# Turning x2 and the gated values: squares of 32 on VectorE and DMAs in runs of 128 B in place of TensorE transposes

## The chip, the cores and the metric

One core of a Trainium2 chip runs the whole program. The metric is the device time of one execution in microseconds (us). "PE" is TensorE, "DVE" is VectorE, "ACT" is ScalarE, "POOL" is GpSimd and "SP" is SyncE, whose queue issues most DMAs.

## The reference, cut to what matters

One layer of a hybrid decoder in float32, 512 positions and 2048 channels: norm, one wide projection, attention and RWKV-7 heads, a gated merge, then

```python
    x = x + merged @ w_out[l]                                   # x2
    h = rms_norm(x, norm_ffn[l])
    x = x + (jax.nn.silu(h @ ffn_gate[l]) * (h @ ffn_up[l])) @ ffn_down[l]
    return rms_norm(x, norm_final)
```

`FFN_HIDDEN` is 5632. The change concerns what stands between these products: x2 (the first line's sum) and the gated values silu(..) * (..) have to be turned, one with channels on the partitions into positions on the partitions, the other the opposite way, because a matmul contracts over the partitions.

## The kernel before, in words

**Precision.** Each float32 product is made of three matmuls: an operand is split by ACT into a rounded high part and by DVE or POOL into the low rest, and high x high, high x low and low x high are summed in PSUM.

**The output projection.** 16 tiles of 128 channels (m = 0 to 15), 48 matmuls of 128x512 each. For a tile, POOL makes the low part of the weights (`low_part`), DVE adds the residual (`residual`, L1708) into one of two x2 buffers, ACT scales and squares it, and DVE builds the sums that the FFN needs. PE then turns the tile in four 128x128 transposes (`turn_x2`, L2399), ACT copies the bank to `xt` and writes it to `sum_dram` (`turned_x2`, L1089), which holds the residual with positions on the partitions; the end of the FFN is added there.

**The FFN.** It is computed by a scheme of seven products of half-size blocks, in the order (1, 7, 5, 6, 2, 3, 4), with sums before and after. There are 11 chunks of 512 hidden columns (j = 0 to 10: gate and up), then 6 passes for the down product (j = 11 to 16). In a chunk each product has 8 steps (k), a step is six matmuls of 128x512 (`gate_up_items`, L2419). For every step ACT writes `ring_hi` (`ring_high`, L1055) and DVE `ring_lo` (`ring_low`, L1752); these rings are four deep, and ACT may refill a place only when PE has done the step four before. All queues are programs written out by hand in this order; nothing is scheduled by a tool. I write (5,3) for product 5, step 3.

**The weights.** SP loads four blocks of 2 MB per chunk (`load_block`, L665). POOL issues two further DMAs of 1 MB per chunk that add one block onto another in memory (L791); they start when DVE has made `ring_lo` for (7,3) and (7,7), and product 6 needs them.

**The seam.** While chunk j runs, the results of chunk j - 1 are finished: silu by ACT, the product by DVE (`hidden1` L1801 at the end of the chunk, `hidden2` L1813 in product 7 of the next). These values stand in three buffers of 128x2x512, `u2buf`, `u3buf` and `c22buf`, as positions x hidden columns. PE turns them in 8 transposes after product 4 (`u2buf`) and 8 more after (7,3) of the next chunk (`c22buf`), ACT copies the four banks back (`turned1_out`, `turned2_out`), DVE makes four sums (`s_of_hidden`, L1819), and SP stores the seven operand blocks to `s_dram` in four DMAs. The three buffers are used again by the running chunk: ACT copies product 1 to `u2buf` at (6,4) and (6,5), DVE writes `u3buf` in product 2.

**The down passes.** `s_dram` is read back, 1 MB for each operand block, by `load_s` (L677) at j = 10, 12 and 14, and split by ACT and DVE (`split_s`, `s_low`) in the product after.

## Time and profile before

| | |
|---|---|
| median of 3 runs | 2778.48 us (2775.72 to 2781.59) |
| the profiled execution, its own time | 2777.86 us |
| its span | 2776.0 us |
| PE busy | 2730.2 us |
| DVE, ACT, POOL busy | 1798.3, 1267.3, 639.2 us |
| data moved by DMA | 382.51 MB in 190611 packets |

The span is the time from the first to the last instruction in the profile; what lies around it is 1.9 us. Busy PE time counts matmuls that overlap, so the distance between the starts of two matmuls says more than the length of one.

### The profile page before, as it was taken

How to read it: one execution, taken by the hardware profiler on the slowest of the kernel's cores; microseconds unless marked ns; L12 is line 12 of the kernel's file. 1: busy time of each engine (PE TensorE's matmuls, PEld its weight loads, DVE VectorE, ACT ScalarE, POOL GpSimd, SP SyncE). 2: the span in 40 equal slices, each digit the busy share in tenths (PEclk: the TensorE clock that was granted, in tenths of full speed). 3: DMA queues.
4: the chain of work that ended last, by engine and by line, in shares of the span. 5: the costliest groups of instructions: out<-in, count | busy, mean ns of one | idle time of the engine just before them, and what ended most of it. 6: DMA issues, size and time to landing. Idle time of an engine off the chain costs nothing.

```text
span 2776.0 us, 37866 instructions
## 1 busy us (share of the span) xinstructions
PE 2730.2 (98%) x14290; PEld 2204.4 (79%) x14290; DVE 1798.3 (65%) x2947; ACT 1267.3 (46%) x2110; POOL 639.2 (23%) x487
## 2 busy tenths in 40 slices
PE   8999999999999999999999999999999999999997
PEld 7777777777777777888887888888888888888876
DVE  5656365364463554432258878887788789888886
ACT  5444343343333334222345555555555556556555
POOL 2323234243333343554440000000000000111112
PEclk9999999999999999999999999999999999999999
DMA  5222122222222223443445665446545677787784
GB/s 189 76 76 105 64 84 94 76 88 79 76 84 83 78 97 110 160 155 129 136 132 160 178 178 153 143 160 178 145 130 162 178 215 213 190 255 179 197 215 109
DMA packets 190611, 382.51 MB, mean 138 GB/s; under 512 B 9584, under 2 KB 84592, under 8 KB 175728
## 3 DMA queue, kind: packets, MB, share of 16 engines
q1 hardware_dynamic: 145808, 319.76, 33.3%
q0 software_dynamic: 29728, 45.09, 9.9%
q10 hardware_dynamic: 14912, 15.47, 1.6%
q8 instruction: 103, 1.69, 0.2%
q14 instruction: 60, 0.49, 0.1%
HBM read 328.91 MB, written 51.38 MB: 137 GB/s over the span
## 4 chain that ended last, share of the span: by engine, by line
PE 91%; DVE 3%; ACT 2%; issue 1%; DMA 1%; DVEq 1%; POOL 0%; ACTq 0%; SPq 0%; POOLq 0%
PE dense L2037 12%; PE work L2430 11%; PE work L2432 11%; PE work L2434 11%; PE dense L2039 11%; PE dense L2038 11%; PE dense L2430 3%; PE dense L2432 3%; PE dense L2434 3%; PE work L2205 1%; PE work L2443 1%; PE work L2257 1%; ACT whi L821 1%; DVEq L1313 1%; PE work L2037 1%
## 5 line engine op out<-in xcount | busy, mean ns | idle before, releaser
L821 ACT ACTIVATE ring_hi<-wblock 128x512 fp32r<-128x512 f32 x840 | 529.7, 632 | 526.0 <-PE work L2434 350.2
L759 POOL TENSOR_TENSOR wlo<-raw,whi 128x512 fp32r<-128x512 f32 x400 | 541.1, 1383 | 896.4 <-ACT whi L821 896.4
L1756 DVE TENSOR_TENSOR ring_lo<-wblock,ring_hi 128x512 fp32r<-128x512 f32 x840 | 575.9, 689 | 166.5 <-ACT ring_hi L821 157.7
L2430 PE MATMUL work<-ring_hi,S_hi 128*128 128x512 f32 x1460 | 572.0, 392 | 6.9 <-DVE ring_lo L1756 6.8
L2432 PE MATMUL work<-ring_hi,S_lo 128*128 128x512 f32 x1460 | 568.9, 390 | 0.0
L2434 PE MATMUL work<-ring_lo,S_hi 128*128 128x512 f32 x1460 | 568.8, 390 | 0.0
L2037 PE MATMUL dense<-H_hi,whi 128*128 128x512 f32 x1208 | 504.8, 418 | 10.0 <-DVE H_lo L1341 8.5
L2039 PE MATMUL dense<-H_hi,wlo 128*128 128x512 f32 x1208 | 473.2, 392 | 0.0
L2038 PE MATMUL dense<-H_lo,whi 128*128 128x512 f32 x1208 | 473.0, 392 | 0.0
L821 ACT ACTIVATE whi<-raw 128x2048 fp32r<-128x2048 f32 (+1 forms) x109 | 198.2, 1821 | 473.7 <-PE dense L2039 388.3
L2430 PEld LDWEIGHTS work<-ring_hi,S_hi 128*128 128x128 f32 x1460 | 274.4, 188 | 69.5 <-DVE ring_lo L1756 7.3
L2434 PEld LDWEIGHTS work<-ring_lo,S_hi 128*128 128x128 f32 x1460 | 274.5, 188 | 57.2
L2432 PEld LDWEIGHTS work<-ring_hi,S_lo 128*128 128x128 f32 x1460 | 274.6, 188 | 55.7
L2037 PEld LDWEIGHTS dense<-H_hi,whi 128*128 128x128 f32 x1208 | 227.6, 188 | 81.7 <-issue 27.0
L2039 PEld LDWEIGHTS dense<-H_hi,wlo 128*128 128x128 f32 x1208 | 227.4, 188 | 49.9
L2038 PEld LDWEIGHTS dense<-H_lo,whi 128*128 128x128 f32 x1208 | 228.0, 189 | 44.8 <-issue 5.8
L791 POOL DMA_DIRECT2D wblock<-w_gu x22 | 28.4, 1290 | 799.3 <-DVE ring_lo L1756 799.3
L2430 PE MATMUL dense<-ring_hi,S_hi 128*128 128x512 f32 x388 | 153.0, 394 | 2.4 <-DVE ring_lo L1756 2.1
L2432 PE MATMUL dense<-ring_hi,S_lo 128*128 128x512 f32 x388 | 151.1, 389 | 0.0
L2434 PE MATMUL dense<-ring_lo,S_hi 128*128 128x512 f32 x388 | 151.1, 389 | 0.0
L2037 PE MATMUL dense<-M_hi,whi 128*128 128x512 f32 x256 | 101.1, 395 | 0.0
L2039 PE MATMUL dense<-M_hi,wlo 128*128 128x512 f32 x256 | 99.8, 390 | 0.0
(337 smaller groups left out, 3409.4 us busy)
## 6 DMA issues: line engine op xcount, KB each, us to landing
raw<-w_slots SPq DMA_DIRECT2D x101, 1024.0 KB, 4.9
wblock<-w_gu SPq DMA_DIRECT2D x88, 1024.0 KB, 9.7
wblock<-w_down SPq DMA_DIRECT2D x60, 512.0 KB, 7.1
wblock<-w_gu POOLq DMA_DIRECT2D x22, 1024.0 KB, 9.9
S_raw<-s_dram SPq DMA_DIRECT2D x14, 1024.0 KB, 7.5
tight<-w_down SPq DMA_DIRECT2D x20, 512.0 KB, 8.6
gates_dram<-gout ACTq DMA_DIRECT2D x32, 256.0 KB, 2.1
gin<-gates_dram SPq DMA_DIRECT2D x16, 512.0 KB, 3.7
```

What stands on the lines that cost most here:

```text
L759: done = nc.gpsimd.tensor_tensor(wlo[s][:, at], raw[s][:, at], whi[s][:, at].bitcast(f32), SUB)
L791: pool.dma_start(into, src, accum_op=ADD).then_inc(t2_added[h], 16)
L821: return A.activation(dst, src, ACT.Copy, scale=scale)
L1313: V.drain()
L1756: V.tensor_tensor(ring_lo[w % RING][:], of_tile(j, source[product], k), ring_hi[w % RING][:].bitcast(f32), SUB).then_inc(ring_lo_ready, 1)
L2037: PE.matmul(bank[:], whi[s][:, wk], hi[:, k, :], start=(k == first), stop=False)
L2038: PE.matmul(bank[:], whi[s][:, wk], lo[:, k, :], start=False, stop=False)
L2039: done = PE.matmul(bank[:], wlo[s][:, wk], hi[:, k, :], start=False, stop=(k == last))
L2205: done = PE.matmul(g_bank(2 * t + e)[:, half:half + 2 * P], src[heads[e], tok], zq[heads[e], t].rearrange("p a n -> p (a n)"), start=True, ...
L2430: PE.matmul(banks[a][:], S_hi[product][:, k, tok], high[:], start=(k == 0 and product not in (3, 2)), stop=False, skip_group_check=True)
L2432: PE.matmul(banks[a][:], S_lo[product][:, k, tok], high[:], start=False, stop=False, skip_group_check=True)
L2434: done = PE.matmul(banks[a][:], S_hi[product][:, k, tok], rest[:], start=False, stop=(k == depth(j) - 1), skip_group_check=True)
```

## The change

The 64 transposes of x2 and the 176 of the gated values go from PE, and ACT's copies of their banks with them. DVE turns instead, and turns only squares of 32x32 within a buffer of 128x512: each square is transposed where it stands. DMAs then put the squares in their places. Since a square has rows of 32 values, every run is 128 B.

- For x2, DVE writes `xt`, ACT stores it to a new `x2_dram`, and in chunks 1 to 8 SP moves it from there to `sum_dram`, 64 DMAs of 32x16 runs in all (`move_x2`), behind the stores of the seam.
- For the gated values there are four turns of 128x512 per chunk, and the sums are made of turned squares. The seven operand blocks are stored in 28 DMAs of 32x16 runs of 128 B, where 4 DMAs in runs of 2 KB were.
- `s_dram` is laid out in rows of four squares, so that `load_s` reads runs of 512 B, four DMAs for each block.
- The semaphores follow: DVE's last sum waits for the stores of products 1 and 2 (8 DMAs), ACT's copy of product 1 waits for those of products 5 and 7.

```diff
-            def store_s(j, product, buf, stored):
-                cols = slice(j * CHUNK_F, (j + 1) * CHUNK_F)
-                rows = s_dram[S_ROWS[product]:S_ROWS[product] + 2][:, :, cols]
-                sp.dma_start(rows.rearrange("a p c -> p a c"), buf[:]).then_inc(stored, 16)
+            def store_s(j, product, piece, stored):
+                cols = s_dram[S_ROWS[product]][:, 4 * j * CHUNK_F:4 * (j + 1) * CHUNK_F]
+                placed = cols.rearrange("i (x q n) -> q i x n", q=4, n=32)
+                for q in range(4):
+                    sp.dma_start(placed[q], piece[32 * q:32 * (q + 1), :].rearrange("i (x n) -> i x n", n=32)
+                                 ).then_inc(stored, 16)
...
-                sp.dma_start(S_raw[product][:, 0:count, :], cols.rearrange("p (k t) -> p k t", t=HALF_T)
-                             ).then_inc(s_loaded[product], 16)
+                found = cols.rearrange("i (x b n) -> b i x n", b=4, n=P)
+                for b in range(4):
+                    into = S_raw[product][32 * b:32 * (b + 1), 0:count, :]
+                    sp.dma_start(into.rearrange("i k (s n) -> i (k s) n", n=P), found[b]
+                                 ).then_inc(s_loaded[product], 16)
...
+            def move_x2(m):
+                rows = sum_dram[:].rearrange("t p c -> (t p) c").rearrange(
+                    "(b i) (m q n) -> m q i b n", i=32, q=4, n=32)
+                turned = x2_dram[m].rearrange("(q i) (b n) -> q i b n", i=32, n=32)
+                for q in range(4):
+                    sp.dma_start(rows[m, q], turned[q]).then_inc(x2_moved, 16)
...
                 if 0 < j <= CHUNKS:
+                    sp.wait_ge(c_ready, part(j - 1, "t2"))
+                    store_s(j - 1, 4, u3buf[:, 1, :], s64_stored)
+                    sp.wait_ge(c_ready, part(j - 1, "t1"))
+                    store_s(j - 1, 2, c22buf[:, 1, :], s12_stored)
+                    store_s(j - 1, 1, c22buf[:, 0, :], s12_stored)
                     sp.wait_ge(c_ready, part(j - 1, "sa"))
-                    store_s(j - 1, 5, c22buf, s57_stored)
-                    sp.wait_ge(c_ready, part(j - 1, "sb", 0))
-                    store_s(j - 1, 6, u3buf, s64_stored)
-                    sp.wait_ge(c_ready, part(j - 1, "sb", 1))
-                    sp.dma_start(s_dram[S_ROWS[3]][:, (j - 1) * CHUNK_F:j * CHUNK_F], u2buf[:, 1, :]
-                                 ).then_inc(s3_stored, 16)
+                    store_s(j - 1, 5, u2buf[:, 0, :], s57_stored)
+                    store_s(j - 1, 7, u2buf[:, 1, :], s57_stored)
+                    sp.wait_ge(c_ready, part(j - 1, "sb"))
+                    store_s(j - 1, 6, u3buf[:, 0, :], s64_stored)
+                    store_s(j - 1, 3, c22buf[:, 1, :], s3_stored)
+                if 1 <= j <= HK:
+                    sp.wait_ge(xt_stored, 16 * KD)
+                    move_x2(2 * j - 2)
+                    move_x2(2 * j - 1)
...
                             if seam:
-                                act.wait_ge(s12_stored, 16 * j)
-                                act.wait_ge(s3_stored, 16 * j)
+                                act.wait_ge(s57_stored, S_PAIR * j)
...
+            def turn_x2(m):
+                if m:
+                    dve.wait_ge(xt_stored, 16 * m)
+                V.transpose(xt[:], x2[m % 2][:]).then_inc(x2_turned, 1)
...
+            def turn_hidden(into, hidden, half):
+                fence()
+                V.transpose(into[:, half, :], hidden[:, half, :]).then_inc(c_ready, 1)
...
+                if i == 3:
+                    dve.wait_ge(s12_stored, S_PAIR * (j + 1))
+                    fence()
+                    V.tensor_tensor(c22buf[:, 1, :], c22buf[:, 1, :], u3buf[:, 0, :], SUB).then_inc(c_ready, 1)
...
-                gate_up_items(j, 7, range(4))
-                if seam:
-                    pe.wait_ge(c_ready, part(j - 1, "hid2"))
-                    turn_hidden(bank_b, c22buf).then_inc(hid_turned, 1)
-                gate_up_items(j, 7, range(4, n))
+                gate_up_items(j, 7, range(n))
```

`S_PAIR` is 128, the count that 8 DMAs leave. `fence()` makes DVE finish its writes before the next instruction reads them. Left out above are the removed `turn_x2` and `turn_hidden` of PE, ACT's copies, and the views that let buffers be written in the order of the squares.

DVE's program in chunk 1 from (5,2) on, before; `ring_lo` and `ring_hi` with their numbers are the ring's four places, and lines L1823 to L1832 are `s_of_hidden`:

```order
1059 L1756 TENSOR_TENSOR ring_lo_198<-wblock_188,ring_hi_194 128x512
1060 L1756 TENSOR_TENSOR ring_lo_199<-wblock_188,ring_hi_195 128x512
1061 L1823 TENSOR_TENSOR c22buf<-u3buf 128x512
1062 L1756 TENSOR_TENSOR ring_lo_196<-wblock_188,ring_hi_192 128x512
1063 L1825 TENSOR_TENSOR c22buf<-u2buf,u3buf 128x512
1064 L1756 TENSOR_TENSOR ring_lo_197<-wblock_188,ring_hi_193 128x512
1065 L1828 TENSOR_TENSOR u3buf<-c22buf,u2buf 128x512
1066 L1756 TENSOR_TENSOR ring_lo_198<-wblock_188,ring_hi_194 128x512
1067 L1832 TENSOR_TENSOR u2buf<-u2buf,u3buf 128x512
1068 L1756 TENSOR_TENSOR ring_lo_199<-wblock_188,ring_hi_195 128x512
```

The same place in the changed program, from (5,3) to (6,2); the other three turns stand behind (5,0), (5,1) and (5,2):

```order
1079 L1764 TENSOR_TENSOR ring_lo_199<-wblock_188,ring_hi_195 128x512
1080 L1834 STREAM_TRANSPOSE c22buf<-u2buf 128x512
1081 L1764 TENSOR_TENSOR ring_lo_196<-wblock_188,ring_hi_192 128x512
1082 L1840 TENSOR_TENSOR u2buf<-u3buf 128x512
1083 L1764 TENSOR_TENSOR ring_lo_197<-wblock_188,ring_hi_193 128x512
1084 L1842 TENSOR_TENSOR u2buf<-c22buf,u3buf 128x512
1085 L1764 TENSOR_TENSOR ring_lo_198<-wblock_188,ring_hi_194 128x512
1086 L1845 TENSOR_TENSOR u3buf<-u2buf,c22buf 128x512
1087 L1764 TENSOR_TENSOR ring_lo_199<-wblock_188,ring_hi_195 128x512
1088 L1764 TENSOR_TENSOR ring_lo_196<-wblock_189,ring_hi_192 128x512
1089 L1764 TENSOR_TENSOR ring_lo_197<-wblock_189,ring_hi_193 128x512
1090 L1849 TENSOR_TENSOR c22buf<-c22buf,u3buf 128x512
```

The sums come one step later each, and the fourth, which overwrites what products 1 and 2 store from, has moved from behind (5,6) to behind (6,1).

SP's queue between two chunks, before:

```order
154 L675 DMA s_dram<-u2buf 128x2x512
155 L675 DMA s_dram<-c22buf 128x2x512
156 L675 DMA s_dram<-u3buf 128x2x512
157 L720 DMA s_dram<-u2buf 128x512
158 L669 DMA wblock_188<-w_gu 128x4x512 x2
```

And now (the name `x_dram` is `x2_dram`):

```order
154 L688 DMA s_dram<-u3buf 32x16x32 x4
155 L688 DMA s_dram<-c22buf 32x16x32 x8
156 L688 DMA s_dram<-u2buf 32x16x32 x8
157 L688 DMA s_dram<-u3buf 32x16x32 x4
158 L688 DMA s_dram<-c22buf 32x16x32 x4
159 L717 DMA sum_dram<-x_dram 32x16x32 x8
160 L681 DMA wblock_188<-w_gu 128x4x512 x2
```

Ahead of the next chunk's first weights stand 36 DMAs instead of 4.

## Rows read from the trace of the kernel before

**Rows 1.** The page's first part: busy time, share of the span, instructions.
```profile
PE 2730.2 (98%) x14290; PEld 2204.4 (79%) x14290; DVE 1798.3 (65%) x2947; ACT 1267.3 (46%) x2110; POOL 639.2 (23%) x487
```
**Rows 2.** The chain that ended last, its share by engine.
```profile
PE 91%; DVE 3%; ACT 2%; issue 1%; DMA 1%; DVEq 1%; POOL 0%; ACTq 0%; SPq 0%; POOLq 0%
```
**Rows 3.** Stretches: us, PE, PEld, DVE, ACT, POOL busy, clock, DMA share, GB/s.
```profile
1544.66:1622.91 78.25, 78.24 (x356) 64.67 (x354) 63.60 (x99) 40.79 (x67) 2.56 (x2) 1.00 0.55 159
1321.06:1332.42 11.36, 11.36 (x54) 9.38 (x53) 2.09 (x4) 3.70 (x6) 5.22 (x4) 1.00 0.43 138
...
2400.00:2470.00 70.00, 70.00 (x310) 57.78 (x309) 60.19 (x95) 39.48 (x66) 8.55 (x7) 1.00 0.84 224
```
**Rows 4.** The transposes' line, L2443: ns min/median/max, first and last start, us.
```profile
L2443 PE MATMUL work<-cst,u2buf x88: 270/272/273, 1543.9 to 2327.1; 128*128 128x128 f32 x88
...
L2443 PE MATMUL work<-cst,c22buf x88: 272/273/273, 1561.4 to 2344.6; 128*128 128x128 f32 x88
```
**Rows 5.** PE in order of time around 8 transposes: start, length, instruction.
```profile
1543.41 0.39 PE L2432 MATMUL work<-ring_hi,S_lo 128*128 128x512 f32 x1
1543.64 0.39 PE L2434 MATMUL work<-ring_lo,S_hi 128*128 128x512 f32 x1
1543.87 1.03 PE L2443 MATMUL work<-cst,u2buf 128*128 128x128 f32 x8
1544.66 0.48 PE L2430 MATMUL dense<-ring_hi,S_hi 128*128 128x512 f32 x1
1544.98 0.40 PE L2432 MATMUL dense<-ring_hi,S_lo 128*128 128x512 f32 x1
```
**Rows 6.** PE in order of time around the four transposes of one x2 tile.
```profile
1332.11 0.60 PE L2405 MATMUL work<-cst,x 128*128 128x128 f32 x4
1332.46 0.48 PE L2037 MATMUL dense<-M_hi,whi 128*128 128x512 f32 x1
1332.78 0.40 PE L2038 MATMUL dense<-M_lo,whi 128*128 128x512 f32 x1
```
**Rows 7.** DVE in order of time, `ring_lo` of (5,1) and (6,1), idle time before in brackets.
```profile
1565.92 0.69 DVE L1756 TENSOR_TENSOR ring_lo<-wblock,ring_hi 128x512 fp32r<-128x512 f32 x1 [0.67 <-ACT ring_hi L821]
...
1576.80 0.69 DVE L1756 TENSOR_TENSOR ring_lo<-wblock,ring_hi 128x512 fp32r<-128x512 f32 x1 [0.67 <-ACT ring_hi L821]
```
**Rows 8.** PE in order of time: the first matmul of (6,2).
```profile
1581.31 0.39 PE L2430 MATMUL work<-ring_hi,S_hi 128*128 128x512 f32 x1
```
**Rows 9.** ACT in order of time: (6,4) and product 1's first copy behind it.
```profile
1580.21 0.63 ACT L821 ACTIVATE ring_hi<-wblock 128x512 fp32r<-128x512 f32 x1 [0.73 <-PE work L2434]
1580.75 0.58 ACT L821 ACTIVATE u2buf<-dense 128x512 f32<-128x512 f32 x1
```
**Rows 10.** POOL in order of time: the first adding DMA of chunk 1.
```profile
1560.13 1.28 POOL L791 DMA_DIRECT2D wblock<-w_gu  x1 [72.16 <-DVE ring_lo L1756]
```
**Rows 11.** DMA queue q0 (POOL's) in 1562 to 1571, then in 1574 to 1575.
```profile
q0 software_dynamic: 769, 1.54, 106.5%
...
q0 software_dynamic: 15, 0.02, 11.9%
```
**Rows 12.** Both queues in 2484 to 2487: packets, MB, share of 16 engines.
```profile
q0 software_dynamic: 221, 0.45, 80.9%
q1 hardware_dynamic: 221, 0.23, 28.0%
```
**Rows 13.** One store of `xt` alone: queue in 1439.4 to 1440.3, and its time to landing.
```profile
q10 hardware_dynamic: 527, 0.26, 96.7%
...
L1096 ACTq DMA_DIRECT2D sum_dram<-xt x1: 367/367/367, 1438.5 to 1438.5; - x1
...
DMA to landing us min/median/max: 2.2/2.2/2.2
```
**Rows 14.** Queue in 1.7 to 2.2: the load of `norm_g`, 24 KB in 128 runs.
```profile
q1 hardware_dynamic: 144, 0.02, 28.6%
```
**Rows 15.** Waits for `s_dram` read back: us in total, times, longest us.
```profile
ACT S_hi L821 <- DMA S_raw<-s_dram: 4.1, 3, 1.7
```

More of the change, by code:

```diff
@@ L515, in resid_of, with rows_of, like_rows @@
             return resid[m // CT][:, m % CT, :]
+        def rows_of(j, buf, a):
+            if j >= CHUNKS:
+                return buf[:, a, :]
+            return buf[:].rearrange("p x (c s n) -> p (x c) s n", s=2, n=P)[:, :, a, :]
+        def like_rows(j, ap):
+            return ap[:] if j >= CHUNKS else ap[:].rearrange("p (c n) -> p c n", n=P)
         def bank_of(j, product):
@@ L1206, in _ @@
                     for e in events(j, k):
-                        if seam and e in (3, 4):
-                            turned1_out(j - 1, e - 3)
                         if seam and e in (6, 7):
@@ L1223, in _ @@
                     ring_high(j, 5, k)
-                    if seam and k in (1, 2):
-                        turned2_out(j - 1, k - 1)
                     if j == 0 and k == 4:
                         s_late(2)
+                        store_x2(KD - 1)
                     split_s(j, 5, k)
@@ L1896, in _ @@
                     ring_low(j, 5, k)
+                    if j == 0 and k == 2:
+                        turn_x2(KD - 1)
                     if k:
@@ L1900, in _ @@
                         s_late_low(1, 2)
-                    if seam and k in (3, 4, 5, 6):
-                        s_of_hidden(j - 1, k)
+                    if seam and k in (0, 1):
+                        turn_hidden(u3buf, c22buf, k)
+                    if seam and k in (2, 3):
+                        turn_hidden(c22buf, u2buf, k - 2)
+                    if seam and k in (4, 5, 6):
+                        s_of_hidden(j - 1, k - 4)
                     if last and k in (2, 3):
@@ L1911, in _ @@
                     s_low(j, *((6, k - 1) if k else (5, n - 1)))
+                    if seam and k == 1:
+                        s_of_hidden(j - 1, 3)
                     if j == 0 and k == 5:
@@ L2444, in turn_halves @@
                 return done
-            def turn_hidden(banks, buf):
-                return turn_halves(banks, [buf[:, a, :] for a in range(2)])
             def s_wait(j, product):
@@ L2456, in _ @@
             for j in range(LAST):
-                n, seam, down = depth(j), 0 < j <= CHUNKS, j >= CHUNKS
+                n, seam = depth(j), 0 < j <= CHUNKS
                 if j:
@@ L2480, in _ @@
                     pe.wait_ge(ms_ready, 2)
-                elif seam:
-                    pe.wait_ge(c_read, copied(j - 1, "out1"))
                 else:
@@ L2486, in _ @@
                 gate_up_items(j, 5, range(n))
-                if seam:
-                    pe.wait_ge(c_read, copied(j - 1, "out2"))
-                elif j:
+                if j:
                     pe.wait_ge(c_ready, part(j - 1, "c21"))
-                else:
-                    pe.wait_ge(xt_copied, KD + 1)
                 s_wait(j, 6)
@@ L2508, in _ @@
                 gate_up_items(j, 4, range(n))
-                if not down:
-                    pe.wait_ge(c_ready, part(j, "hid1"))
-                    turn_hidden(bank_d, u2buf).then_inc(hid_turned, 1)
             def turn_fin(n, b):
```

134 lines of the change are left out of this document (50 added, 84 removed).

## The prediction

> **What bounds the kernel now.** I read the page first: PE is busy for 98% of the span [rows 1], and the chain that ended last is PE for 91% of its length [rows 2]. The table of stretches then shows that this holds where the change works: in a chunk of 78.25 us PE is busy for 78.24, DVE for 63.60, ACT for 40.79, and the DMA engines for 0.55 of the time; a tile of the output projection takes 11.36 us with PE busy throughout; a down pass keeps the DMA engines at 0.84 [rows 3]. So a microsecond taken from PE is a microsecond of the program, as long as nothing arrives later than now. The granted clock is 1.00 in all three rows, the 2.4 GHz level. I then looked for what arrives last in the seam: the timeline of DVE, PE and ACT in products 5 and 6 [rows 7 to 9] and the DMA queues there [rows 10, 11].
>
> **What goes from PE.** Matmuls of 128x512 start 0.227 us apart (1543.41 and 1543.64). Eight transposes stand between 1543.64 and 1544.66, that is 1.02 us where 0.23 would be, so 0.79; the matmul after starts 0.32 later instead of 0.23, so 0.09 more: 0.88 us for eight [rows 5]. There are 88 + 88 transposes, 22 such groups [rows 4]: 22 x 0.88 = 19.4 us. For x2, four transposes start at 1332.11 and the next matmuls at 1332.46 and 1332.78: 0.35 + 0.09 = 0.44 us [rows 6]; 16 tiles give 7.0 us. PE is the bound in both places, so all 26.4 us count. ACT loses four copies of some 0.58 us per chunk; it has 37 us of slack there, worth nothing.
>
> **What comes to DVE.** 44 + 16 turns of 128x512. No row shows one; the nearest is another 128x512 instruction, 0.69 us [rows 7], and I bound it by half and twice that. In product 5, where the four stand, DVE is idle 0.67 us before each step [rows 7], and `ring_lo` of (6,1), ready at 1577.5, is used by PE 2.5 us later: (6,2) starts at 1581.31 and a step is six matmuls, 1.36 [rows 8]. Four turns with their fences overrun the gaps by some 0.2 us each, less than that lead: zero. At twice the price they would overrun by 0.9 each, 3.6 us in all, and leave about 1 us of stall per chunk, 11 us. In the output projection DVE works 2.09 us of 11.36 [rows 3]: zero.
>
> **What comes to the queues, and the new waits.** This term decides. A chunk now stores 28 x 512 = 14336 runs of 128 B, 896 for each of the 16 DMA engines, plus one semaphore packet per DMA. The fourth sum on DVE, behind (6,1), waits until the 8 DMAs of products 1 and 2 have landed; 4 DMAs of product 4 stand ahead of them, so 12 x 33 = 396 packets per engine. Behind this wait is `ring_lo` of (6,2), and PE waits for it. ACT's copy of product 1 behind (6,4) waits for 8 DMAs more, 660 packets per engine; behind it is `ring_hi` of (6,5).
>
> When can they start? DVE's (5,1) starts at 1565.92 [rows 7], now 0.88 earlier without the transposes after (7,3); with the turn and its fence behind it, the first stores are issued at 1566.5. A store alone was issued at 1438.5, ran in 1439.4 to 1440.3 and landed 2.2 us after its issue [rows 13]: 0.9 us to the first packet, 0.4 after the last. So they run from 1567.4. But POOL's two adding DMAs, the first issued at 1560.13 [rows 10], fill the engines then: 769 packets in 9 us, a packet per engine each 0.187 us, and the last 15 in 1574 to 1575 [rows 11]; they end at 1574.2. When both queues have work they take turns packet by packet, whatever the size: 221 packets of 2 KB against 221 of 1 KB in the same 3 us [rows 12]. So until 1574.2 an engine passes only 37 of the small packets. The Trainium skill, in "DMA: Bandwidth & Descriptors" (Queues, rings and completion order), says that an engine changes queue only after a packet of typically 9 to 17 descriptors; if SP's packets held up to twice as many as POOL's, some 37 more would be through by then and the stall below would be about 0.5 us shorter per chunk, 6 us in all. The equal counts in the row give no sign of it, so the sum goes by one for one.
>
> After 1574.2 the price p of one small packet counts. The stores of products 5 and 7 have passed at 1574.2 + (660 - 37) p and landed 0.4 later; behind the wait ACT needs 0.58 for the copy and 0.63 for `ring_hi` [rows 9], DVE 0.69 for `ring_lo`, against PE's start of (6,5) at 1581.31 - 0.88 + 3 x 1.36 = 1584.5. Stall = 623 p - 8.0 us. The first wait, with two DVE instructions and a fence (1.5 us) behind it and PE's (6,2) at 1580.4, gives 359 p - 4.3, which is the smaller from p = 14 ns on. Before, the copy began at 1580.75 with no wait.
>
> For p, the nearest rows: 144 packets of 24 KB, 171 B on average, took 28.6% of 16 engines for 0.5 us, 15.9 ns each [rows 14]; 527 of 0.26 MB, 497 B, took 96.7% for 0.9 us, 26.4 ns each [rows 13]. A line through both gives **14 ns** at 128 B. The first is a load and not a write to memory, the second is. Upper bound from rows: the price of a 512 B write, 26.4 ns, in case there is a floor per packet. I take 14: the nearest row in size is the first, and at 512 B the time an engine is busy and the time between packets are the same (96.7%), so nothing else limits the feed. At 14 ns the stall is 0.7 us per chunk, 11 x 0.7 = 7.7.
>
> **Chunk 10 and the read back.** In chunk 10 the block of product 7 is read back ahead of the stores, now 4 x 33 packets of 512 B: 37 pass under POOL's DMAs and 95 x 26.4 ns = 2.5 us are added to both waits: 2.5. In passes 12 and 14, seven blocks each, a MB costs 132 x 26.4 ns = 3.5 us of an engine's time; now three short waits for it take 4.1 us together [rows 15]. Bounds: nothing if hidden, and 14 x 1.7 = 24 if half of each were exposed. With DMA at 0.84 [rows 3] I take 4, as much as stands there now.
>
> **The moves of x2.** 64 DMAs, 264 packets per engine and chunk, have no row of their own. At 14 to 53 ns (twice the 512 B write, for reading and writing) they take 4 to 14 us of the 35 us in which the engines rest per chunk. They stand before the next chunk's first weights, which are needed at about 1617; at p = 14 ns they are through by 1601. Zero. ACT's store of `xt` is as large as before.
>
> **The sum.** -19.4 - 7.0 + 7.7 + 2.5 + 4 = -12.2 us. Against the profiled execution, 2777.86, that is 2765.7, so **2766 us**; the median of the runs is 0.6 above this execution, which I leave out. The forecast's own range is 2755 to 2773, p from 12 to 15 ns.
>
> **The rivals.** What a measurement of this kernel can tell from no change is about 0.2%, 5.5 us: 2773 to 2784.
>
> A: the stores land in time (p at most 12 ns, or the sums' wait is met), and the read back is hidden: -26.4, 2751 us. For it: engines are busy little over half the time. Against it: the queue is full exactly from 1562 to 1574.
>
> B, slower: the wait of ACT for the stores of products 5 and 7 takes the place of the transposes. A packet of 128 B costs as much as one of 512 B, 26.4 ns. Stall 623 x 0.0264 - 8.0 = 8.4 us, and the stall by DVE's wait, 5.2, lies within it; 11 x 8.4 = 92.7; with -26.4 + 2.5 + 4 that is +73, 2851 us. It decides from p = 15.8 ns on, where the sum is zero; each ns more costs 6.9 us. For it: all writes in short runs that the trace shows are of 512 B, and none is cheaper. Against it: the load of `norm_g` is.
>
> C: a short write costs more than a long one. The Trainium skill states in the Specifications of "DMA: Bandwidth & Descriptors" that below 512 B an engine reads, modifies and writes. As a mechanism of this kernel: the engine handles each run twice, 2 x 26.4 = 53 ns. Stall 25 us per chunk, 275 in all, 3033 us; and 896 + 256 runs at 53 ns are 61 us beside the 43 that an engine is busy per chunk now (0.55 x 78.25), so DMA itself would bound chunks 1 to 8. No row shows a short write to memory; the load of `norm_g` into SBUF shows no such doubling.
>
> D: the gain is given back in the down passes, where loads in 512 B take turns with POOL's adding DMAs: +20 more than I took, 2786 us.
>
> That the transposes do not go is no case; they are gone from the program.
>
> **How the numbers follow.** Forecast 0.37, A 0.10, near no change (p between 15 and 17) 0.07, D 0.05, B with its neighbours from 17 to 30 ns 0.26, C 0.15. Faster: 0.37 + 0.10 = 0.47; same 0.07 and a part of D, 0.09; slower 0.44. The range runs from A's side, 2748, to a little above B, 2872; it leaves out C and a few in a hundred. Cases of both signs hold much, so the likeliest one's own range stands above.
>
> **What would show it.** Right: chunks of about 77.2 us instead of 78.25; tiles of 10.9; the stores' queue showing about 14 ns per packet; DVE's fourth sum and ACT's copy behind (6,4) waiting for DMA s_dram, PE idle under 1 us per chunk before `ring_lo`. Wrong: a chunk longer than 78.3, with ACT `u2buf` waiting for the stores for several us, or PE waiting for weights; DVE turns above 1.2 us; waits for S_raw above 10 us in the passes.

## The result and the profile after

The change takes 2799.57 us, median of four runs (2792.71 to 2799.75), against 2778.47 (four runs, 2775.72 to 2781.59): ratio 1.0071, 95% interval 1.0057 to 1.0086, so 0.7% slower. In a later set it took 2800.47. I had forecast 2766 us with 0.47 for faster. The profiled execution is the fastest of the four, 2792.71 with a span of 2790.9; that span exceeds before's by 14.8 us, where the medians differ by 21.

The page of the changed kernel, first part and the chain by engine:
```profile
PE 2718.1 (97%) x14050; PEld 2177.6 (78%) x14050; DVE 1826.9 (65%) x3007; ACT 1232.9 (44%) x2050; POOL 639.4 (23%) x487
PE 75%; DVE 11%; SPq 4%; ACT 3%; issue 2%; DMA 2%; DVEq 2%; POOL 0%; ACTq 0%; POOLq 0%
```
PE has lost 12 us of work against [rows 1], but the chain is PE for 75% only, where it was 91% [rows 2]; DVE has 11%, and SP's queue, which had nothing, 4%.

The table of stretches, after: an output projection tile (from its first matmul to that of the next), chunk 2, pass 12 (us, PE, PEld, DVE, ACT, POOL busy, clock, DMA share, GB/s):
```profile
1318.53:1329.41 10.88, 10.88 (x50) 9.01 (x49) 2.73 (x4) 3.20 (x4) 5.23 (x4) 1.00 0.40 145
1617.35:1696.20 78.85, 77.52 (x337) 62.69 (x336) 65.17 (x103) 38.36 (x62) 2.55 (x2) 1.00 0.67 163
2412.68:2490.92 78.24, 76.63 (x338) 62.91 (x336) 65.31 (x103) 43.11 (x72) 10.03 (x8) 1.00 1.01 233
```
A tile takes 10.88 us where it took 11.37, as forecast. A chunk is without its 16 transposes and is longer than in [rows 3] all the same: PE is idle for 1.33 us of it. Chunk starts, read off PE's timeline, give the account. The first chunk starts 8.5 us earlier: 7.3 from the tiles, and 1.2 that arose before the first tile, where nothing was changed. Chunk 0 is 1.55 shorter, chunk 1 is 4.5 longer (82.74), chunks 2 to 9 are 0.3 to 1.2 longer each (6.6 in all), chunk 10 is 4.9 longer (83.17), and passes 11 to 16 take 457.8 us where they took 448.9: +8.9. Together +14.8.

The waits of the change (us in total, times, longest):
```profile
PEld work L2439 <- DVE ring_lo L1764: 46.2, 46, 3.2
ACT u2buf L845 <- DMA s_dram<-u2buf: 45.7, 10, 6.6
DVE c22buf L1849 <- DMA s_dram<-c22buf: 33.3, 10, 3.9
PE work L2439 <- DVE ring_lo L1764: 32.8, 39, 4.7
ACT S_hi L845 <- DMA S_raw<-s_dram: 14.9, 4, 4.7
ACT ring_hi L845 <- DMA tight<-w_down: 11.5, 2, 7.4
```
The third and second are the two waits that the prediction had built its stall on; the fifth answers to [rows 15], 4.1 us before. PE waits for `ring_lo` behind all of these. The last is a load of weights in pass 15. It is the largest single piece of the passes' loss: ACT waits 7.4 us for it where it waited 4.6 at most before, PE stops for 4.9 us in product 5 where it stopped for 1.5, and the pass takes 83.4 us in place of 79.5.

ACT, then DVE and PE in order of time in product 6 of chunk 2:
```profile
1657.46 0.60 ACT L845 ACTIVATE u2buf<-work 128x512 f32<-128x512 f32 x1 [4.27 <-DMA s_dram<-u2buf]
...
1653.10 0.69 DVE L1849 TENSOR_TENSOR c22buf<-c22buf,u3buf 128x512 f32<-128x512 f32 x1 [3.27 <-DMA s_dram<-c22buf]
...
1654.45 0.50 PE L2439 MATMUL work<-ring_hi,S_hi 128*128 128x512 f32 x1 [0.64 <-DVE ring_lo L1764]
...
1659.36 0.50 PE L2439 MATMUL work<-ring_hi,S_hi 128*128 128x512 f32 x1 [0.49 <-DVE ring_lo L1764]
```
DVE's fourth sum stands 3.27 us idle for the stores of products 1 and 2, ACT's copy 4.27 for those of 5 and 7. PE stops once behind each: the matmuls ahead of these two started at 1653.43 and 1658.48, so the starts lie 1.02 and 0.88 us apart where 0.23 is usual. Waits of 3.3 and 4.3 us thus cost PE under 2 us; the rest is lead, steps whose operands already stood in the rings.

Where the stop is longer, it costs more than its own length. In chunk 1 ACT waited 6.56 us, PE's starts lay 3.12 us apart (a stop of 2.9), and then came a stretch at the lower of the clock's two levels, 0.50 of full speed or 1.2 GHz:
```profile
1579.80:1583.20 3.40, 3.40 (x10) 2.63 (x9) 2.47 (x5) 0.98 (x2) 0.00 (x0) 0.50 0.52 83
```
Seven matmuls in it start 0.43 us apart in place of 0.23, 1.4 us in all; behind the stop of 4.9 us in pass 15 it is nine. After the stops of chunk 2 there are none.

SP's queue in order of time, the 28 stores of chunk 2 (start, us over all of them, times):
```profile
1640.28 5.07 SPq L688 DMA_DIRECT2D s_dram<-u3buf  x4
1645.39 6.20 SPq L688 DMA_DIRECT2D s_dram<-c22buf  x8
1651.64 4.32 SPq L688 DMA_DIRECT2D s_dram<-u2buf  x8
1656.00 2.15 SPq L688 DMA_DIRECT2D s_dram<-u3buf  x4
1658.19 2.17 SPq L688 DMA_DIRECT2D s_dram<-c22buf  x4
```
Here is what I had not costed. Once POOL's adding DMAs have ended, SP issues a store every 0.54 us (4.32 / 8), one directly behind the other. While they run, it takes 1.3 us for one (5.07 / 4).

The DMA queues in 1652.1 to 1655.9, where only these stores run. The first line is the busy share of the 16 engines, in tenths, in 40 slices; the last one gives the stores' time to landing:
```profile
DMA  3999504999407997218997029995059993079981
q1 hardware_dynamic: 3697, 0.46, 70.5%
s_dram<-u2buf SPq DMA_DIRECT2D x8, 64.0 KB, 1.9
```
3697 packets of 128 B in 3.8 us on 16 engines: one every 16.4 ns, of which an engine is busy 11.6. The engines work in bursts and rest between two stores. So a short packet is cheaper than the 14 ns I took, and the pace is slower.

DVE in order of time in (7,1) and (7,2), with PE's stop behind it:
```profile
1629.84 0.75 DVE L1828 SCALAR_TENSOR_TENSOR c22buf<-c22buf,rstd,u3buf 128x512 f32<-128x512 f32 x1
1630.50 0.69 DVE L1764 TENSOR_TENSOR ring_lo<-wblock,ring_hi 128x512 fp32r<-128x512 f32 x1
1631.10 0.69 DVE L1795 TENSOR_TENSOR wblock<-wblock,wblock 128x512 f32<-128x512 f32 x1
1631.70 0.75 DVE L1828 SCALAR_TENSOR_TENSOR c22buf<-c22buf,rstd,u3buf 128x512 f32<-128x512 f32 x1
...
1633.11 0.50 PE L2439 MATMUL dense<-ring_hi,S_hi 128*128 128x512 f32 x1 [0.21 <-DVE ring_lo L1764]
```
DVE has no gap here: gated values of the second hidden half (L1828) stand between the ring's parts and make it late. The eight transposes that stood behind (7,3) were time in which it caught up.

### The profile page after: what moved, and what is told of

Read it like the earlier page. It is cut to its first block, busy times and chain, and to the rows that moved or that the text cites. A ratio compares the mean times of both kernels' runs of the same rounds, so it can differ in the third digit from the quotient of the medians.

```text
span 2790.9 us, 37811 instructions
## 1 busy us (share of the span) xinstructions
PE 2718.1 (97%) x14050; PEld 2177.6 (78%) x14050; DVE 1826.9 (65%) x3007; ACT 1232.9 (44%) x2050; POOL 639.4 (23%) x487
## 4 chain that ended last, share of the span: by engine, by line
PE 75%; DVE 11%; SPq 4%; ACT 3%; issue 2%; DMA 2%; DVEq 2%; POOL 0%; ACTq 0%; POOLq 0%
PE dense L2061 12%; PE dense L2063 11%; PE dense L2062 11%; PE work L2439 8%; PE work L2443 8%; PE work L2441 8%; SPq L688 3%; DVE ring_lo L1764 3%; DVEq L1317 2%; DVE wblock L1795 2%; PE dense L2439 2%; PE dense L2441 2%; PE dense L2443 2%; PE work L2229 1%; DVE wblock L1789 1%
## 5 line engine op out<-in xcount | busy, mean ns | idle before, releaser
L1764 DVE TENSOR_TENSOR ring_lo<-wblock,ring_hi 128x512 fp32r<-128x512 f32 x840 | 569.2, 686 | 126.7 <-ACT ring_hi L845 120.3
L2443 PE MATMUL work<-ring_lo,S_hi 128*128 128x512 f32 x1460 | 569.7, 390 | 0.0
L2443 PEld LDWEIGHTS work<-ring_lo,S_hi 128*128 128x128 f32 x1460 | 274.9, 188 | 58.0
L2443 PE MATMUL dense<-ring_lo,S_hi 128*128 128x512 f32 x388 | 151.6, 391 | 0.0
L2062 PE MATMUL dense<-M_lo,whi 128*128 128x512 f32 x256 | 99.6, 389 | 0.0
```

The source lines that it names most:

```text
L1764: V.tensor_tensor(ring_lo[w % RING][:], of_tile(j, source[product], k), ring_hi[w % RING][:].bitcast(f32), SUB).then_inc(ring_lo_ready, 1)
L2062: PE.matmul(bank[:], whi[s][:, wk], lo[:, k, :], start=False, stop=False)
L2443: done = PE.matmul(banks[a][:], S_hi[product][:, k, tok], rest[:], start=False, stop=(k == depth(j) - 1), skip_group_check=True)
```

## The experiments

All ratios are against the kernel before, measured beside each kernel (2777.2 to 2778.0 us). Intervals are 95%. Differences in us are of medians, against the change's 2800.47. In the runs with other run lengths, fewer DMAs or another read back, values land in other places, so they show times only.

### The change again

> The changed kernel once more, on the chip of the three runs beside it: 2793 to 2800 us, and the same two gaps of product 6 and one of product 7 in every chunk. It tells how far the three ratios can be compared with the first measurement of the change.

Measured: 2800.47 us (2793.95 to 2804.90), 1.0082 (1.0062 to 1.0103). The gaps stand where they stood. Single executions of the change differ by 11 us; before's beside it lie within 5. The profiled execution, 2798.0 us, is 5.3 above the first one. Of this, 3.1 us are in the chunks and 2.6 in pass 15 (86.0 us in place of 83.4). Thirteen more matmuls start 0.43 us apart, 7 in chunk 9 and 6 in pass 15; that is 2.6 us.

### The buffers asked for later

In the seams only, ACT's copies of product 1 move from (6,4), (6,5) to (6,6), (6,7), and DVE's fourth sum from (6,1) to (6,3).
```diff
-                        if e in (4, 5):
+                        late = 2 if seam else 0
+                        if e in (4 + late, 5 + late):
...
-                    if seam and k == 1:
+                    if seam and k == 3:
                         s_of_hidden(j - 1, 3)
```


> In the change, product 6 now runs 1.5 to 2.3 us per chunk over what its matmuls take (5.7 and 6.0 in chunks 1 and 10), where product 4 had lost 0.8 before. Theory 1: this is the wait of ScalarE's copy into u2buf at (6,4) and of VectorE's fourth sum into c22buf at (6,1) for stores that SyncE issues one every 0.54 us (28 of them, 15.1 us, behind each chunk's start). This run asks for both buffers two steps (7.4 us) later and changes nothing else: the two gaps of product 6 vanish in chunks 2 to 9, 9 x about 2.0 us, and most of the 5.7 and 6.0 us in chunks 1 and 10, together 20 to 28 us: 2772 to 2779 us, ratio about 0.997 to the kernel before. Theory 2: the short packets slow the other transfers or the engines' writes, and the waits only show it; then the time stays within 5 us of the change's 2799. Theory 3: the turns on VectorE make it late by themselves; then the gaps move to other steps of product 6 and under 8 us come back.

Measured: 2772.86 us, 0.9981 (0.9972 to 0.9991); 27.6 us come back. (A step is 1.36 us, so two steps are 2.7 us and not the 7.4 of the expectation.) Chunk 7 in the table of stretches, and one of the waits:
```profile
1999.71:2076.80 77.09, 76.89 (x337) 62.85 (x336) 65.44 (x103) 38.40 (x62) 2.58 (x2) 1.00 0.69 168
```
```profile
ACT u2buf L845 <- DMA s_dram<-u2buf: 18.9, 9, 3.2
```
The stores are as many and as short as before the move, and the chunk is 1.16 us shorter than in [rows 3]. ACT still waits, 18.9 us over nine chunks in place of 45.7 over ten, and PE has no gap in product 6 in six of the eight chunks 2 to 9: a wait of 2 us no longer reaches it. Theory 2, that the short packets cost the time by themselves, falls. Chunk 10 keeps 4.2 us in product 6.

### The second hidden half later in product 7

```diff
-                    if seam and k in (1, 2):
-                        hidden2(j - 1, k - 1)
+                    if seam and k in (6, 7):
+                        hidden2(j - 1, k - 6)
```


> In product 7 of every chunk TensorE now waits about 0.6 us for VectorE's low part of the ring, which it did before too, but then 8 transposes stood behind (7,3) and the operands caught up in them. Theory 1: VectorE is full in the first steps of product 7 because the two sums of the second hidden half (0.7 to 1.4 us each) fall in (7,1) and (7,2). This run does them in (7,6) and (7,7), one thing changed: the 0.9 us over the matmuls' own time in product 7 fall below 0.3, 11 x 0.6 = 6.6 us back, 2792 us. As the stores of a chunk wait for the turned copies of these sums, product 6's waits may grow by what the stores come later; then the time stays at 2799 or rises. Theory 2: the wait is one for ScalarE or for a store; then product 7 keeps its 0.9 us.

Measured: 2791.73 us, 1.0046 (1.0029 to 1.0063), 8.7 below the change beside it. Chunk 2:
```profile
1608.50:1686.60 78.10, 76.79 (x337) 62.72 (x336) 64.85 (x103) 38.30 (x62) 2.55 (x2) 1.00 0.67 165
```
Product 7 takes 0.1 us over its matmuls' time in place of 0.9, and PE's waits for `ring_lo` in it are gone. Waits in product 6 stay (45.0 and 35.3 us in all): next to nothing is handed on. This was DVE's lateness. In the kernel before, product 7 took 12.07 us with its transposes and takes 11.78 without them: only 0.3 of their 0.88 us came free, the rest had lain under them.

### Both

> Both moves together: buffers asked for two steps later in product 6, and the second hidden half summed in (7,6) and (7,7). Theory 1, in which both losses are times at which VectorE or ScalarE is late and the two are independent: 2799 - 24 - 6.6 = about 2768 us, between 2763 and 2775, so under the kernel before (2778), by 0.1 to 0.5%. If the short packets themselves cost the time: not under 2790. If both losses have the same slack behind them (what is taken away in product 7 reappears in product 6): about 2776, as with the later waits alone.

> The version with both moves once more, in more rounds: 2768 us, ratio 0.996, against 2770.8 and 0.9975 for the x2 part alone, so that the gated part with its waits moved takes no more than the transposes it replaces. If the first measurement was a lucky one, it comes out at 2771 or more, level with the x2 part alone.

Measured: 2768.02 us, 0.9958 (0.9941 to 0.9974), then 2767.17 us in five rounds, 0.9963 (0.9949 to 0.9976). Chunk 3 of the second:
```profile
1688.88:1765.20 76.32, 76.32 (x338) 62.98 (x336) 65.15 (x103) 38.50 (x62) 2.56 (x2) 1.00 0.69 168
```
PE is busy throughout, the chunk is 1.93 us shorter than before. That is the prediction's 2 x 0.88 = 1.76 and a little more. The two gains nearly add: 27.6 and 8.7 us one by one, 32.5 together.

### Longer runs, same number of DMAs

```diff
-                placed = cols.rearrange("i (x q n) -> q i x n", q=4, n=32)
+                placed = cols.rearrange("i (q y) -> q i y", q=4)
...
+                    sp.dma_start(placed[q], piece[32 * q:32 * (q + 1), :]).then_inc(stored, 16)
```


> The change with each of its 28 stores per chunk written as 32 runs of 2 KB in place of 512 runs of 128 B: same 28 DMAs, same 64 KB each, same reads and waits; the values land in other places, so the shares read back are of wrong columns and the output isn't the reference's. Theory 1 (SyncE's issue of 0.50 us per DMA with its 512 runs is what the buffers wait for): the issue of such a DMA gets much shorter, all 28 are out within some 5 us, and both gaps of product 6 vanish as in the run with the later waits: 2772 to 2779 us, product 7 as in the change. Theory 2 (28 DMAs cost their time whatever their runs are, 0.5 us each): the gaps stay and the time is 2799. The passes show whether their 9 us come from the short stores of the chunk before (then pass 11 alone is shorter) or not.

Measured: 2773.74 us, 0.9981 (0.9972 to 0.9991). The time is that of theory 1, its ground is not: SP's issues of products 5 and 7 in chunk 2, and the waits,
```profile
1644.21 3.71 SPq L688 DMA_DIRECT2D s_dram<-u2buf  x8
```
```profile
DVE c22buf L1848 <- DMA s_dram<-c22buf: 6.1, 9, 2.4
ACT u2buf L844 <- DMA s_dram<-u2buf: 7.7, 10, 1.6
```
show 0.46 us per DMA in place of 0.54. The 28 stores did not go out in 5 us. The last store that ACT waits for was issued by 34.9 us after the chunk's start and not by 38.6; that was enough. The passes kept their loss, so it does not come from the length of the stores' runs.

A point between, 256 runs of 256 B (`n=64` in place of `n=32` in both lines of `store_s`):

> The change with each of its 28 stores per chunk written as 256 runs of 256 B in place of 512 runs of 128 B (same DMAs, bytes and waits; values land in other places, so the output isn't the reference's). With 32 runs of 2 KB the time was 2774 and both gaps of product 6 were gone; with 512 runs a DMA is issued every 0.54 us and the gaps are 2.0 us per chunk. Theory 1 (the pace is SyncE's issue, which grows with the runs): about 0.4 us per DMA, the last store a buffer waits for lands some 2 to 3 us earlier, the gaps fall from 2.0 to 0.3 us or less in chunks 2 to 9: 2774 to 2780. Theory 2 (what counts is that a run is under 512 B): as with 128 B, 2790 or more.

Measured: 2774.07 us, 0.9990 (0.9980 to 0.9999). SP's queue:
```profile
1634.31 2.86 SPq L688 DMA_DIRECT2D s_dram<-u3buf  x4
...
1643.55 3.99 SPq L688 DMA_DIRECT2D s_dram<-u2buf  x8
```
0.50 us per DMA, not the 0.4 expected, and the waits in this chunk are 1.2 and 1.7 us against 3.3 and 4.3, with no gap of PE in product 6. These 20 stores go out in 13.2 us in place of 15.7, and most of that came from the first four, those issued beside POOL's adding DMAs (2.86 against 5.07).

### Fewer DMAs, same runs

Products 2 and 1 leave in four DMAs of 1024 runs of 128 B, and so do 5 and 7: 20 DMAs per chunk.
```diff
-                    store_s(j - 1, 2, c22buf[:, 1, :], s12_stored)
-                    store_s(j - 1, 1, c22buf[:, 0, :], s12_stored)
+                    store_pair(j - 1, 0, c22buf, s12_stored)
...
+                    sp.dma_start(placed[q], buf[32 * q:32 * (q + 1), :, :].rearrange("i a (x n) -> i (a x) n", n=32)
```


> What is known: 28 stores of 64 KB are issued every 0.50 us with 512 runs, 0.46 with 256, 0.42 with 32; VectorE's and ScalarE's longest typical waits in chunk 2 are 3.3 and 4.3, 1.2 and 1.7, 0.5 and 0.4 us, and TensorE loses 2 us per chunk only in the first. Open is whether the number of DMAs, of runs or of bytes sets the pace. This run stores products 2 and 1 by 4 DMAs of 128 KB with 1024 runs of 128 B each, and 5 and 7 likewise: 20 DMAs per chunk in place of 28, same bytes, same runs (shares of 1, 2, 5 and 7 land elsewhere, the output isn't the reference's). Theory 1, number of DMAs (0.42 us each whatever is in it, 0.08 us for 512 runs): about 0.6 us per double DMA, so that the last of products 5 and 7 is issued 8 x (1.0 - 0.6) = 3 us earlier; gaps of product 6 vanish, 2774 to 2780. Theory 2, number of runs or bytes: about 1.0 us per double DMA, nothing moves, 2799.

Measured: 2786.08 us, 1.0023 (1.0014 to 1.0033): half of what the later waits gave. SP's queue and the waits:
```profile
1637.14 5.40 SPq L690 DMA_DIRECT2D s_dram<-u3buf  x4
1642.59 4.52 SPq L698 DMA_DIRECT2D pair_dram<-c22buf  x4
1647.15 3.02 SPq L698 DMA_DIRECT2D pair_dram<-u2buf  x4
```
```profile
DVE c22buf L1860 <- DMA pair_dram<-c22buf: 32.4, 10, 4.3
ACT u2buf L856 <- DMA pair_dram<-u2buf: 3.5, 1, 3.5
```
A double DMA takes 0.75 us where two singles took 1.08: of the 0.54, by these two, 0.33 is for the DMA and 0.21 for its 512 runs and 64 KB. ACT's wait is gone. DVE's is not: its stores come first, beside the end of POOL's adding DMAs, and there 4 DMAs in place of 8 save 1.7 us only, while a double store takes 3.4 us from issue to landing where a single one took 1.9. So both have a part, number and contents; bytes and runs aren't told apart.

### A second engine issues

The 8 DMAs of products 5 and 7 go to ACT's queue, two behind each of (6,0) to (6,3).
```diff
-                    store_s(j - 1, 5, u2buf[:, 0, :], s57_stored)
-                    store_s(j - 1, 7, u2buf[:, 1, :], s57_stored)
...
+                    if seam and k < 4:
+                        store_57(j - 1, k)
```


> The change with the 8 DMAs that store the shares of products 5 and 7 issued from ScalarE's queue, two each behind its work of (6,0) to (6,3), in place of SyncE's. Theory 1 (the pace is that of one engine's issue, 0.54 us per DMA): ScalarE's own wait before (6,4) (4.3 us in chunk 2) vanishes or falls under 1 us, VectorE's wait at its fourth sum (3.3 us in chunk 2, for stores that SyncE issued ahead of these) stays, ScalarE pays 8 x 0.5 = 4 us of issuing where it has slack; product 6 keeps about half of its 2.0 us: 2799 - 10 = 2789, between 2784 and 2794. Theory 2 (the pace is that of the DMA engines, which both queues share): the landing of the last store is as late as before, and the time stays at 2799 or rises by up to 4 us x 11.

Measured: 2824.02 us, 1.0175 (1.0155 to 1.0196), 24 us slower than the change. The expectation missed by 35 us. Queues in 1648 to 1652 of chunk 2, then the waits:
```profile
q1 hardware_dynamic: 2971, 0.37, 68.5%
q10 hardware_dynamic: 2722, 0.34, 62.2%
```
```profile
DVE c22buf L1858 <- DMA s_dram<-c22buf: 55.9, 11, 6.4
ACT u2buf L842 <- DMA s_dram<-u2buf: 24.8, 11, 3.0
```
With two issuing, 5693 packets pass in 4 us, one every 11.2 ns per engine, and the engines are busy for 90% or more in each of 40 slices of these 4 us: now they are the bound, as theory 2 has it. The queues take turns (2971 against 2722, as in [rows 12]), so ACT's stores, which nobody needed first, took half the engines from those that DVE waits for: its wait rose from 33.3 to 55.9 us. SP's slow pace lies a third below this, and the order within one queue was worth more than a second issuer.

The waits are not all of the loss. In chunk 3 PE's starts lie 4.00 us apart in (6,2), and the clock is at its lower level behind it:
```profile
1738.60:1744.70 6.10, 6.08 (x14) 4.79 (x15) 2.47 (x4) 1.57 (x3) 0.00 (x0) 0.50 0.63 106
```
In chunks 1 to 10 of this run 64 matmuls start 0.43 us apart, in the change 7. That is 57 x 0.2 = 11 us, of the 26 by which these chunks are longer in the profiled execution.

### The read back

First four DMAs with runs of 8 KB, then one DMA with runs of 8 KB on 128 partitions, whose edit is
```diff
-                for b in range(4):
-                    into = S_raw[product][32 * b:32 * (b + 1), 0:count, :]
-                    sp.dma_start(into.rearrange("i k (s n) -> i (k s) n", n=P), found[b]
+                into = S_raw[product][:, 0:count, :]
+                sp.dma_start(into.rearrange("i k t -> i (k t)"), cols.rearrange("i (b y) -> i b y", b=4)
...
```


> The change with the shares of the first factors read back by 4 DMAs of 32 runs of 8 KB in place of 4 DMAs of 512 runs of 512 B; the values land in other places, so the products use wrong columns. Nothing else differs. Theory 1: the passes are near the bound of their transfers (DMA busy 0.84 there), the shares now come in 512 B where they came in longer runs, and that is the 9 us by which passes 11 to 16 grew: they fall to within 2 us of the kernel before, total 2789 to 2793, chunks 0 to 10 as in the change (chunk 1 up to 2 us shorter). Theory 2: the passes' loss comes from the end of the last chunk's stores or from the changed start alone; then they keep at least 6 of their 9 us.

Measured: 2795.86 us, 1.0059 (1.0042 to 1.0076). Passes 11 to 16 take 460.6 us: nothing of their loss comes back, so the 512 B run is not its cause.

> The change with each share read back by one DMA of 128 runs of 8 KB onto 128 partitions, as in the kernel before, in place of four DMAs on 32 partitions each (values in other places, output not the reference's). Long runs in four DMAs brought nothing back in the passes (11 to 16: 460.6 us against the change's 457.8 and before's 449.1). Theory 1: it is the number of DMAs, whose issues stand in a full queue ahead of the other loads; then ScalarE waits for S_raw under 6 us in all (14.9 in the change, 4.1 before), and the passes fall by 4 to 7 us, down to the 2 us which VectorE's turns in pass 11 cost: 2790 to 2795. Theory 2: the reads are late because the chunks' stores ahead of them were; then passes 12 to 16 keep their length, 2799.

Measured: 2785.74 us, 1.0039 (1.0023 to 1.0054). Pass 12 in the table of stretches:
```profile
2410.45:2486.76 76.31, 76.31 (x337) 62.99 (x336) 65.40 (x103) 43.25 (x72) 10.04 (x8) 1.00 0.87 247
```
76.31 us as before, and the passes take 451.1 (the medians differ by 14.7 us, the profiled executions by 8.6). The longest wait for the weights in `tight` is back at 4.6 us, and pass 15 at 79.8. What is left is pass 11 (79.3 against 77.7), where DVE makes the last turns and is busy for 73 of 79 us; PE stops for its `ring_lo` in product 5, where the turns stand. Packets of SP's queue in pass 12, with four DMAs of long runs and with one:
```profile
q1 hardware_dynamic: 10062, 14.21, 63.6%
```
```profile
q1 hardware_dynamic: 10191, 14.93, 55.4%
```
About the same number of packets, the loads of weights included, and fewer bytes: the engines are busy for 0.636 x 16 x 77.98 / 10062 = 79 ns each against 66. What differs is that a block is read in four DMAs, each of which reaches 32 partitions and not 128. The Trainium skill states in "SBUF — State Buffer" (Door 1: The DMA port swizzle) that 32 partitions are reached through 8 of 16 ports only, and ("Can I just issue two DMAs to hit both halves?") that two transfers aren't joined to use both halves; a longer time per packet is what that would give. The trace agrees as far as it goes: it shows no ports. The expectation had put the loss down to the number of DMAs; that and the spread over partitions were not taken apart.

### x2 alone

The kernel before with the change's part on x2.

> The kernel before with the part of the change on x2 alone: x2 turned in squares by VectorE, its squares stored and moved by DMA in runs of 128 B, gated values turned by TensorE as before. In the change's trace the first chunk starts 8.5 us earlier and the chunks with moves (1 to 8) are no longer than chunk 9 without. Theory 1: the x2 part brings 8.5 us and its moves cost nothing: 2770 us, between 2767 and 2773, ratio 0.997. Theory 2: the moves' short packets collide with what the chunks load: then chunks 0 to 8 are longer than before's 78.25 and the time is 2775 to 2785.

Measured: 2770.83 us, 0.9975 (0.9965 to 0.9985). Chunk 2, with moves of 8 x 512 runs in it:
```profile
1615.33:1693.58 78.25, 78.24 (x355) 64.66 (x354) 63.45 (x99) 40.86 (x67) 2.55 (x2) 1.00 0.59 165
```
The chunk has before's length to the hundredth. The part brings 6.8 us, and its moves cost nothing that shows.

### One more move of order

In chunk 10 the read of product 7's share goes behind the stores of 4, 2 and 1.
```diff
                 load_s(j, 1)
-                load_s(j, 7)
+                if j != CHUNKS - 1:
+                    load_s(j, 7)
...
                     store_s(j - 1, 1, c22buf[:, 0, :], s12_stored)
+                    if j == CHUNKS - 1:
+                        load_s(j, 7)
```


> The version with both moves (2768 us) and one more: in chunk 10 SyncE waits for the end of product 7 and issues 4 DMAs for the pass's share of product 7 ahead of the 28 stores, whose first is issued 28.6 us after the chunk's start there and 23 us in other chunks. Here these four come behind the stores of products 4, 2 and 1. Expected: chunk 10 loses 3.6 us in product 6 and keeps at most 1.5 of it; in pass 11 nothing gets later: 2765.5 us, between 2763 and 2768. Should ScalarE, which waits 5.1 us for a share in chunk 10 already, come to wait for this one by as much longer, the time stays at 2768.

Measured: 2773.89 us, 0.9988 (0.9979 to 0.9997), 6 us slower than with both moves.
```profile
ACT S_hi L848 <- DMA S_raw<-s_dram: 20.8, 4, 10.4
```
Chunk 10 took 86.87 us in place of 80.49: ACT waited 10.4 us for this share, where 5.1 was its longest. It came out the second way and worse. The read had been late already, and 12 matmuls behind PE's stop of 7.3 us started 0.43 us apart.

## Why the prediction was wrong

**The sum against the runs.** Predicted -19.4 -7.0 +7.7 +2.5 +4. Three terms failed: the price of a packet in the stores' waits, which by itself turned the sign, the transposes counted in full, and the read back.

- *-19.4 for 22 groups of transposes.* Each group was priced rightly from [rows 5], but "PE is the bound in both places, so all 26.4 us count" fails for the eleven groups behind (7,3), of which 0.6 of 0.88 us did not come free. With the stores' waits moved away the chunk is 77.09 against 78.25: 1.16 per chunk, 12.8 in all. The missing 7 us are DVE's lateness in product 7, which the second group had covered; moved, they came back (-8.7). The view to read was what follows the removed work on PE: whether the operand of the next step was ready when it began, not only whether PE was busy.
- *-7.0 for x2*: -6.8, by the run with this part alone. Right, moves included.
- *Turns on DVE at nothing.* A turn takes 0.71 us, 0.70 for x2 (L1724, 16 turns, median 701 ns), against 0.69 assumed:
```profile
L1834 DVE STREAM_TRANSPOSE u3buf<-c22buf x22: 711/712/716, 1555.4 to 2356.0; 128x512 f32<-128x512 f32 x22
```
  They fit into product 5 as said. In pass 11, which I had not looked at, they cost 1.9 us.
- *+7.7 and +2.5 for the stores' waits.* This is the step that turned the sign: 27.6 us by the run that asks for the buffers later, against 10.2. The mechanism and both waits stood. So did the turns between the queues: in 1562 to 1563, beside POOL's first adding DMAs, 98 packets of SP's queue passed and 97 of POOL's. The formula stood on average: 623 p - 8.0 us with the measured 16.4 ns is 2.2 us, or 24 + 2.5 in all. Chunks 2 to 9 lost 79.07 - 77.10 = 1.97 on average, chunk 10 6.1, and chunk 1, from whose rows the formula was made, 5.6. There ACT's copy began 3.7 us after the last of its stores was issued, in chunk 2 1.5; what held that store up stays open. That the total fits so well is in part luck. The size of p was wrong, and by what it was read from: "at 512 B the time an engine is busy and the time between packets are the same, so nothing else limits the feed". At 512 B the row was near the engines' limit; at 128 B the engine is busy for 11.6 ns only, and what sets the pace is the issue, a store of 33 packets per engine every 0.54 us. I multiplied packets and never DMAs. My own row would not have been enough, though: the store of [rows 13] took 0.37 us to issue, and 33 packets at 14 ns are 0.46, so by rows the issue would have stayed hidden. (The line through the two rows gives 14.5 ns at 128 B and not 14, 3.4 us more in the sum.) The prediction's threshold, 15.8 ns, was crossed by 0.6 ns.
- *+4 for the read back*: 7 of the 8.9 us of the passes, by the read in one. It was priced by 512 B runs, which cost nothing that could be found; four transfers on 32 partitions each did. It was also looked for in the wait for the blocks alone: 3.9 us of it came as a longer wait for weights, in pass 15.

With the measured sizes: -12.8 - 6.8 + 27.6 + 8.9 = +16.9, between the profiled execution's 14.8 and the median's 21.1. The rest of 4 us is not accounted for; the slower profiled execution of the change, the repeated run's, spends more in product 6 of single chunks and in pass 15, and more matmuls of it run at the clock's lower level. The prediction has no term for the clock, which it had read at 1.00 where PE never stopped.

**The rivals.** B named the right wait and the right side, but its cause, 26.4 ns per short packet, is refuted. The measured p, 16.4 ns, lies in the case "near no change" (15 to 17), for which the prediction's sum gives 2782 us. That the time is 2800 comes from the transposes (+6.6), the read back (+4.9) and the 4 us not accounted for. C is refuted: where the stores run alone, a 128 B write keeps an engine busy for less than half of the 26.4 ns of a 512 B one. (Beside POOL's adding DMAs the record gives 27 ns for it: 73 packets and 3.1% of 16 engines in 1641 to 1645.) The Trainium skill's statement on read-modify-write below 512 B (Specifications of "DMA: Bandwidth & Descriptors") shows in no packet time of the stores alone. D came in part. A would have needed the issue at the engines' pace. One for one between queues held three times: [rows 12], in the change, and between SP's queue and ACT's.

**How the gain can be had.** With two waits and two sums moved, the change is 0.4% faster than before, 2767 us. The x2 part alone gives 2771. The intervals (0.9949 to 0.9976 and 0.9965 to 0.9985) overlap, so that the gated part pays by itself even then isn't settled. Not tried: the read back in one DMA with every value in its place, for which the stores would have to be laid out in another way.

## What to carry to other kernels

Cost a split transfer by its issues as well as by its packets: number of DMAs times the interval at which one engine issues them, against the moment at which a buffer is asked for again; and cost it on both ends, since the four-way split made the read back longer as well. Where work is taken from the engine that is the bound, look at the step behind it: if its operand arrives just in time, part of the removed work was cover. If a new wait costs more than was gained, move the point at which it is asked before changing the transfer: two steps (2.7 us) gave back 27.6 us, a second issuing engine took 24. And count a stop of PE of several us with what follows it: after 2.9 and 4.9 us the matmuls behind ran at 1.2 GHz, for 1.4 and 1.8 us more.

## What the runs showed of the hardware

- A 128 B packet to DRAM keeps a DMA engine busy for 11.6 ns where the stores run alone, and for 27 ns beside POOL's adding DMAs; two queues together pass one every 11.2 ns per engine, one queue with 64 KB DMAs one every 16.4 ns.
- The interval between 64 KB DMAs on SP's queue is 0.54, 0.50 and 0.46 us with 512, 256 and 32 runs, and 0.75 us for 128 KB with 1024 runs: sixteen times fewer runs save 15%.
- Beside POOL's adding DMAs an issue on SP's queue takes longer, 1.3 us per store in place of 0.54; what holds it up, no row shows.
- Queues take turns packet by packet, whatever the size: 98 packets of 128 B against 97 of 2 KB in 1 us, and 2971 against 2722 between SP's queue and ACT's.
- In pass 12 a packet of SP's queue, weights included, keeps an engine busy for 79 ns with a block read in four DMAs onto 32 partitions each, and for 66 ns with one DMA onto 128.
- Behind PE's stops of 2.9 us in chunk 1 and 4.9 us in pass 15 the granted clock was 0.50, and matmuls of 128x512 started 0.43 us apart in place of 0.23; behind stops of under 1 us in chunk 2 it stayed at 1.00.
- DVE turns the squares of 32 in a 128x512 f32 tile at nearly the price of a subtraction of that shape: 0.71 us against 0.69.
